# Window-buffer copies of a decoder step: six under way at once on the sync queue, and ten behind the second sample's dilated rows

## The reference, cut to what matters

```python
ext_k = jnp.concatenate([cache_dil_k[layer], kb_s], axis=1)
ext_v = jnp.concatenate([cache_dil_v[layer], vb_s], axis=1)
...
dk_s.append(ext_k[:, DEC_SEQ:]); dv_s.append(ext_v[:, DEC_SEQ:])
```

## Time and profile before

| what | before |
|---|---|
| median of 3 runs | 1211.17 us (1208.58 to 1219.85) |
| the profiled execution | 1215.47 us |
| its span | 1213.8 us |
| PE busy | 909.9 us (75%) |
| VectorE busy | 635.5 us (52%) |
| bytes moved by DMA | 481.21 MB, mean 396 GB/s |

### The profile page before, as it was taken

One profiled execution on the slowest core, in us unless ns is written; L12 is line 12 of the kernel. 1 busy time (PEld: TensorE's weight loads), 2 busy tenths in 40 slices (PEclk: granted clock), 3 DMA queues, 4 the chain that ended last, 5 costly groups with the idle time before them and its releaser, 6 DMA issues.

```text
span 1213.8 us, 13371 instructions
## 1 busy us (share of the span) xinstructions
PE 909.9 (75%) x3662; PEld 423.6 (35%) x3662; DVE 635.5 (52%) x1604; ACT 351.8 (29%) x959; POOL 420.2 (35%) x430
## 2 busy tenths in 40 slices
PE   2797986668676879964778877877587777777783
PEld 0342443445232448831323322333233322323231
DVE  4200106553222544223776777777777777777755
ACT  0000001463121012221333233323433444244323
POOL 1201323112231000211455554545454455555551
PEclk9799988777898889977999999999999999999996
DMA  9999999988999899999999999999989999999996
GB/s 366 424 379 400 378 365 364 397 338 351 373 392 413 281 367 378 388 396 393 410 414 428 420 428 427 428 428 428 428 357 427 428 427 428 428 428 428 427 427 272
DMA packets 72826, 481.21 MB, mean 396 GB/s; under 512 B 9953, under 2 KB 10306, under 8 KB 27346
## 3 DMA queue, kind: packets, MB, share of 16 engines
q0 software_dynamic: 54720, 377.53, 76.0%
q1 hardware_dynamic: 18066, 103.17, 22.1%
HBM read 477.41 MB, written 70.32 MB: 451 GB/s over the span
## 4 chain that ended last, share of the span: by engine, by line
DMA 46%; PE 30%; issue 8%; DVE 8%; ACT 3%; POOL 2%; SPq 2%; POOLq 0%; DVEq 0%; ACTq 0%
DMA R<-in_uv,idst 29%; PE ps L968 11%; DMA out_dil_v_s<-in_dil_v 6%; DMA R<-in_sb_v,vrow 5%; PE ps L919 5%; PE ps L874 2%; PE ps L576 2%; POOL R L480 2%; DMA R<-in_sb_k 2%; DVE R L1770 2%; DMA vrow<-in_vrow 2%; PE ps L739 2%; PE ps L602 1%; DMA R<-in_uv,idec 1%; ACT wgt L1241 1%
## 5 line engine op out<-in xcount | busy, mean ns | idle before, releaser
L968 PE MATMUL ps<-R,diag 128*128 128x512 f32 x1024 | 491.9, 630 | 168.8 <-ACT diag L1260 167.3
L480 POOL DMA_INDIRECT R<-in_uv,idst x256 | 313.7, 1225 | 365.6 <-PE ps L968 294.6
L1770 DVE CUSTOM_DVE_ANT_0 R<-R,H 128x1024 f32<-128x1024 f32 x264 | 319.3, 1224 | 201.7 <-DMA R<-in_uv,idst 190.7
L968 PEld LDWEIGHTS ps<-R,diag 128*128 128x128 f32 x1024 | 195.7, 199 | 465.0 <-ACT diag L1260 252.0
L1238 ACT ACTIVATE gel<-dots 128x2 f32<-128x2 f32 x132 | 26.8, 203 | 403.9 <-DVE dots L1770 403.9
L576 PE MATMUL ps<-R,HT 128*128 128x512 f32 x192 | 94.3, 631 | 3.9 <-DMA R<-in_wts 3.9
L1260 ACT ACTIVATE diag<-const,wgt 128x128 f32<-128x128 f32 x256 | 88.9, 394 | 14.7 <-PE ps L968 1.4
L310 POOL DMA_INDIRECT R<-in_sb_v,vrow x32 | 30.4, 951 | 114.5 <-PE ps L739 90.2
L432 POOL DMA_DIRECT2D R<-in_wts x24 | 12.8, 541 | 157.3 <-PE ps L874 57.2
L301 POOL DMA_DIRECT2D R<-in_sb_k x64 | 34.7, 542 | 86.5 <-issue 85.9
L1241 ACT ACTIVATE wgt<-gel,gst 128x1 f32<-128x1 f32 x264 | 63.3, 287 | 4.3
(11 more groups left out here) (282 smaller groups left out, 828.6 us busy)
## 6 DMA issues: line engine op xcount, KB each, us to landing
R<-in_wts POOLq DMA_DIRECT2D x48, 1024.0 KB, 17.0
out_dil_k_s<-in_dil_k SPq DMA_DIRECT2D x32, 1023.5 KB
out_dil_v_s<-in_dil_v SPq DMA_DIRECT2D x32, 1023.5 KB
R<-in_sb_k SPq DMA_DIRECT2D x64, 256.0 KB, 8.3
R<-in_sb_k POOLq DMA_DIRECT2D x64, 256.0 KB, 6.7
R<-in_win_v SPq DMA_DIRECT2D x8, 512.0 KB
R<-in_uv,idst POOLq DMA_INDIRECT x256, 11.8
m_all<-in_win_k SPq DMA_DIRECT2D x6, 512.0 KB
```

What stands on the lines that cost most here:

```text
L480: pool.indirect_dma_start(out=R[:, row_slot(k), :], out_offset=None, in_=A["uv"], in_offset=bass.IndirectOffsetOnAxis(ap=idst[:, par, k:k ...
L968: last = pe.matmul(ps[:, banks + q, :], diag[:, k % 4, :], R[:, row_slot(k), D + q * 512:D + (q + 1) * 512], start=False, stop=False, skip ...
L1770: dve.tensor_tensor_reduce(u, u, H[:, t, :], 1.0, 0.0, ALU.mult, ALU.add, dots[:, k:k + 1]).then_inc(s["dot_done"], 1)
```

## The change

The four semaphores become six, and they are taken in turn by the number of the piece: piece n waits for piece n - 6. So up to six pieces are under way at any time. The pieces keep their order (sample by sample, quarter by quarter, keys and values in turn). Ahead of the third sample's dilated value rows stand ten pieces (numbers 16 to 25) in place of four, and after the sub-keys' load 38 in place of 44. The final waits follow the six semaphores. Nothing else changes: `POOL_COPIES` is 0, so GpSimd issues no copy.

```diff
+COPIES = 8 * NB
+EARLY, POOL_FROM, POOL_COPIES, SP_AHEAD = 16, 26, 0, 6
-        copied = [sem(f"copied{n}") for n in range(4)]
+        copied = [sem(f"copied{n}") for n in range(SP_AHEAD)]
+        def copy_piece(eng, n):
+            b, q, m = n // 8, n % 8 // 2, n % 2
+            src, dst = ((A["dil_k"], A["dil_k_s"]), (A["dil_v"], A["dil_v_s"]))[m]
+            size = (PAST - 1) * DG // 4
+            return eng.dma_start(dst[b:b + 1, q * size:(q + 1) * size].rearrange("a (r n) -> (a r) n", r=P),
+                                 src[b:b + 1, q * size + DG:(q + 1) * size + DG].rearrange("a (r n) -> (a r) n", r=P))
-            def copy_piece(pair, odd, m, q):
-                ...
-                landed = copied[2 * odd + m]
-                if not (isinstance(pair, int) and isinstance(q, int) and pair + q == 0):
-                    sp.wait_ge(landed, pair * 64 + q * 16)
-                ...
+            def copies(first, end):
+                for n in range(first, end):
+                    landed = copied[n % SP_AHEAD]
+                    if n >= SP_AHEAD:
+                        sp.wait_ge(landed, 16 * (n // SP_AHEAD))
+                    copy_piece(sp, n if n < POOL_FROM else n + POOL_COPIES).then_inc(landed, 16)
             sp.wait_ge(s["w_used"], 4)
             key_pages(sp, 0, EVEN, first=True)
-            for odd in range(2):
-                copy_windows(0, odd)
+            copies(0, EARLY)
             ...
             for b in range(NB):
                 if b == 2:
-                    copy_windows(1, 0, range(2))
+                    copies(EARLY, POOL_FROM)
             ...
-            copy_windows(1, 0, range(2, 4))
-            for pair, odd in ((1, 1), (2, 0), (2, 1), (3, 0), (3, 1)):
-                copy_windows(pair, odd)
+            copies(POOL_FROM, COPIES - POOL_COPIES)
             ...
-            for n in range(4):
-                sp.wait_ge(copied[n], 16 * 4 * NB // 2)
+            for n in range(SP_AHEAD):
+                sp.wait_ge(copied[n], 16 * len(range(n, COPIES - POOL_COPIES, SP_AHEAD)))
```

More of the change, by code:

```diff
@@ L329, in _ @@
             sp.wait_ge(s["pages_in"], 32)
-            def copy_piece(pair, odd, m, q):
-                src, dst = ((A["dil_k"], A["dil_k_s"]), (A["dil_v"], A["dil_v_s"]))[m]
-                n = (PAST - 1) * DG // 4
-                landed = copied[2 * odd + m]
-                if not (isinstance(pair, int) and isinstance(q, int) and pair + q == 0):
-                    sp.wait_ge(landed, pair * 64 + q * 16)
[L339 to L346, removed]
+            def copies(first, end):
[4 more added lines that the diff above has]
+                    copy_piece(sp, n if n < POOL_FROM else n + POOL_COPIES).then_inc(landed, 16)
             sp.wait_ge(s["w_used"], 4)
             key_pages(sp, 0, EVEN, first=True)
-            for odd in range(2):
-                copy_windows(0, odd)
+            copies(0, EARLY)
             with sp.Fori(1, 4) as b:
```

## The result

The changed kernel takes **1236.6 us** (median of 4 runs, 1234.06 to 1238.65) against 1210.8 us before (median of 4): a ratio of 1.0198, with a 95% interval of 1.0143 to 1.0253. The forecast was 1208 us with a range up to 1221. It was wrong in sign and by 29 us. The profiled execution took 1236.35 us with a span of 1234.6, 20.8 us more than the span before.

The account below looks back on a forecast made before the run. DMA was taken as the bound, with the end set by when the expert gathers get going. From 1215.47 us, -2 + 8 - 8.6 = -2.6 gave 1212.9; that execution being 4.3 over the median, 1208.6, stated as 1208, range 1193 to 1221.

Parts of the forecast that it names:

- the price of a megabyte on GpSimd's queue: Time per megabyte beside six copies under way: 13.7 us, bounds 7.5 and some 20.
- the 14.4 us between two dots: Time from third to fourth expert row before the change, read as the pace with four copies under way.
- Part A: First 16 pieces, beside the q/k/v projection: idle DMA time won, third weight 1 us late; -2 us, bounds -7.4 and +4.
- Part B: Ten pieces at 240.9 us in place of four: 9.3 us fill idle DMA, 9.3 don't; +8 us, bounds 0 and +10.
- Part C: The 38 pieces after the attention: query weights wait behind copies, scores end at 553.4, ninth gather lands at 569.6; -8.6 us.
- The price of a copy: DMA time for one copy piece of 1.048 MB, taken as 3.1 us.
- The idle DMA time: About 16 us before the ninth expert row, all that a deeper or earlier copy stream can fill.
- the fourth: GpSimd's queue starves beyond 13.7 us per megabyte; with 20 us, +11 to +14, 1222 to 1225 us; chance 0.15.
- The third rival: Copies alone still cost 3.4 us a piece with six under way, HBM limiting; 1211 to 1217 us; chance 0.15.
- The second: Weights aren't late, so all idle DMA time is filled; 1191 to 1199 us; chance 0.25.

Follow-up runs that it names:

- early_two: The changed kernel with the first 16 pieces two under way, the later ones still six; 1228.5 us, 1.0163 of the kernel before.
- six_four: The changed kernel with four pieces in place of ten ahead of the third sample's rows, six under way everywhere; 1234.6 us, 1.0202 of the kernel before.
- late_three: As gap_six, but three under way for the last 24 pieces; 1228.0 us, 1.0179 of the kernel before.
- late_four: As gap_six, but four under way for the last 24 pieces; 1228.6 us, 1.0157 of the kernel before.
- gap_six: The changed kernel with six under way only for pieces 16 to 39, two for the first 16 and last 24; 1198.5 us, 0.9914 of the kernel before.
- late_two: The changed kernel with six under way for the first 26 pieces, two for the last 38; 1207.3 us, 0.9991 of the kernel before.

## Why the prediction was wrong

**The step that failed is the price of a megabyte on GpSimd's queue with six copies under way: 13.7 us taken for each weight; in the changed kernel the first query weight took 23.0 us and the next four 15.4 us each (16.1 in early_two and six_four).** A second term was put at nothing: that the copies' own packets take more of the engines' time, 13.3 us in all. The text took the 14.4 us between two dots as "four under way" and lowered it to 13.7 by the rate of that stage. But the four of the earlier trace rows were under way only at the start of those 14.4 us; each of them that landed was not replaced before 536.44, so that the row is a mean from four down to two. The experiments show that three are enough for the full price (15.8 us in late_three), so the row most likely mixes the full price with the low one. The reasoning beside it, that a queue with its next packet always ready gains nothing from more, was right (late_three, late_four and early_two are equal): it should have said that the ceiling lies above a row that dips below it.

Part by part:

- **Part A, -2 forecast, +7.2 measured**, outside its upper bound of +4, with the scatter said above. The text let the weight of 58.14 be the first to meet the copies. The trace after shows that the one before it was still waiting in the queue: PE waits 5.34 us at 79.17 for the projection's fourth slot, and the fifth comes at 96.67, 38 us after its issue. Both the price and the number of megabytes in the queue at 55 us were too low. The wait of 7.44 us for key pages at 120 did go, as the text said it might. With depth two in this place the loss is gone (early_two).
- **Part B, +8 forecast, +10.6 measured** (from +7.2 to +17.8), just outside its upper bound of +10. Its mechanism fits: six more copies in a stretch whose idle time takes three. In six_four, with four pieces, the last value sums start 8.2 us earlier.
- **Part C, -8.6 forecast, +3.0 measured** (from +17.8 to +20.8). The mechanism was right and named as the new wait: weights behind copies, a late score end, idle DMA behind it. Only the size was off. The slots were to begin 13.7 us apart and began 15.4 apart, and the first weight took 23.0 us from its issue (454.20 to 477.18), not 13.7. By the fifth slot that makes 9 us of delay from the first weight and 7 from the four steps behind it. Five slots wait, so the score end was forecast 24 us late on its own shift and came 35 us late. The experts' stage gave 32 of the 53 us back, about what the text had counted on (from 30 us late to 2.6 early).
- **The price of a copy, 3.1 us in all places**, was right for the stretches with copies alone (412 to 436 in gap_six: 3.05 us). But the sum assumed that the copies' time stays the same. The changed kernel's q1 packets take 13.3 us more. In late_two and gap_six, with the last 24 pieces at two, it is 1 and 3 us more than before. In early_two, with six from piece 16 on, it is 11.0 us more, and in late_three, where against gap_six only the last 24 differ, 9.0. So most of it comes with the depth of the late pieces. The text had no term for it.
- **The idle DMA time** of about 16 us was read rightly. gap_six, which fills it without starving, has 12.3 us less of it than the kernel before, and is 0.9% faster.

Of the rivals, the fourth was the nearest: "starvation beyond 13.7 us, decides from about 16 us per megabyte". Its sign, waits of PE in the q/k/v projection between 80 and 110 us, is there (79.17 and 96.67). It put 1222 to 1225 on 20 us and had 15% of the chance; at some 16 us the kernel was already at 1237 us, and the dearer copies and the first weight's 23 us were in none of the cases. So its mechanism was right and its sum was not. The third rival, that copies alone gain no pace, is refuted by the stretch from 412 to 436 in gap_six, 3.05 us a piece. The second, that weights aren't late, is refuted for this packet size. The page of the Trainium skill that it leant on (DMA: Bandwidth & Descriptors, "Queues, rings and completion order") speaks of turns by packets, not by bytes, and the three packet sizes here agree with that in direction: 16.1, 11.5 and at most 7.8 us for a megabyte of the other queue. Strict turns they don't show: an engine moves a megabyte of the other queue in eight packets and a copy piece in one, so one for one would let eight pieces pass, and 4.4 did. I read it as equal halves and so used it against its own wording.

Two rows that the forecast named, a value gather and a value sum, are not among the rows shown ahead of it. They are these, from the kernel before:

```profile
264.38 0.99 POOL L310 DMA_INDIRECT R<-in_sb_v,vrow  x1 [27.87 <-PE ps L739]
```
```profile
288.59 1.92 PE L739 MATMUL ps<-R,ast 128*32 128x512 f32 x16
```

## What to carry to other kernels

A background copy in large packets that shares the DMA engines with loads on a critical path should not keep its queue full: here three pieces under way for the last 24 cost 30 us against two, and six cost no more than three, so for this kernel the step is a threshold and not a slope. Give depth only where the other queue is empty, and move copies into stretches that the windows show idle, up to what these can take. To read the price from a trace, take a stretch in which the depth holds all through it, and look at what stands behind the copies on their own queue as well as on the other.

## What the runs showed of the hardware that I had not expected

- The price on the other queue is at its ceiling with three DMAs under way: weights come 15.8, 15.6 and 16.1 us apart with three, four and six, and the kernels take 1228.0, 1228.6 and 1228.5 us; with two no slot waits at one every 8.4 us, and it is 1198.5.
- A layout that splits an engine's 65,504 contiguous bytes into eight runs makes the HBM to HBM copy slower when it is alone (235 to 271 GB/s against 344), although each run still has 8,188 bytes. Whether the short runs or the distance between them does it was not tried.
- The first weight behind a full copy queue took 23.0 us, the next ones 15.4 each. It is 22 us with three under way too (442.29 to 464.32 in late_three), so it hardly comes from the number of copies under way. Why the first is dearer stays open.
- The same copies in the same bytes took 13 us more of the engines' time when all of them were six deep (281.5 against 268.2 us for q1). Its cause was not separated.
